# Layer 1's weight sums begun behind its own key rotation, and three reordered stretches, in a two-layer encoder step

## What is computed

```
z = rmsnorm(x) @ w_in        # [B | C | xin] conv, [c_q | c_kv | k_rope] attention, [gate_a | gate_b]
y_a = B * causal_conv3(C * xin)
y_b = latent attention of 8 heads with a rotary key, chunk-causal mask
x = x + rmsnorm((sigmoid(gate_a) * y_a + sigmoid(gate_b) * y_b) @ w_o)
x = x + rmsnorm(relu(rmsnorm(x) @ w1)^2 @ w2)
```

## Time and profile before

| what | value |
|---|---|
| median of 3 runs | 1724.19 us (1723.59 to 1724.62) |
| profiled execution | 1722.68 us |
| its span | 1720.9 us |
| TensorE busy | 1700.8 us (99%) |
| VectorE busy | 1324.4 us (77%) |
| ScalarE busy | 868.5 us (50%) |
| GpSimd busy | 142.8 us (8%) |
| DMA: SyncE's queue, GpSimd's queue | 32.2%, 16.4% of the 16 DMA engines' time |

### The profile page before, as it was taken

How to read it: one execution, slowest core, us unless ns; L and a number is a source line. 1 busy time by engine, 2 the same in 40 slices (tenths; PEclk the granted TensorE clock), 3 DMA queues, 4 the chain that set the end, 5 groups by cost and what they waited for, 6 DMA issues and landing times.

```text
span 1720.9 us, 31921 instructions
## 1 busy us (share of the span) xinstructions
PE 1700.8 (99%) x12687; PEld 1684.6 (98%) x12687; DVE 1324.4 (77%) x2538; ACT 868.5 (50%) x1681; POOL 142.8 (8%) x191
## 2 busy tenths in 40 slices
PE   9999999998999999999999999999999999999997
PEld 9999999998999999999999999999999999999997
DVE  7778877777798776668687788777878887777665
ACT  7635454554554454446366364545545536444452
POOL 1421222222000022100001000000000000000000
PEclk9999999999999999999999999999999999999998
DMA  7888888898412488733133234343623313322231
GB/s 239 209 186 183 224 208 219 200 245 241 124 64 70 133 191 180 160 91 106 62 103 133 96 112 132 116 137 108 205 106 99 99 39 109 98 87 86 75 99 56
DMA packets 91733, 233.65 MB, mean 136 GB/s; under 512 B 10304, under 2 KB 21824, under 8 KB 91584
## 3 DMA queue, kind: packets, MB, share of 16 engines
q1 hardware_dynamic: 69184, 179.16, 32.2%
q0 software_dynamic: 21120, 50.34, 16.4%
q10 hardware_dynamic: 1280, 2.10, 0.3%
HBM read 221.20 MB, written 60.69 MB: 164 GB/s over the span
## 4 chain that ended last, share of the span: by engine, by line
PE 90%; DVE 6%; DMA 2%; ACT 1%; issue 1%; SPq 0%; DVEq 0%; ACTq 0%
PE ring L820 18%; PE ring L822 18%; PE ring L821 18%; PE att L820 11%; PE att L822 11%; PE att L821 11%; DVE w_lo L2142 1%; PE att L3683 1%; DMA w_raw<-blocks_in 1%; DVE xs_lo L2561 1%; DMA my<-my_kept 1%; PE att L815 1%; PE att L814 1%; PE att L827 0%; DVE cv L2511 0%
## 5 line engine op out<-in xcount | busy, mean ns | idle before, releaser
L820 PE MATMUL ring<-xs_hi,w_lo 128*128 128x288 f32 x1792 | 532.9, 297 | 2.9 <-issue 1.2
L822 PE MATMUL ring<-xs_hi,w_hi 128*128 128x288 f32 x1792 | 527.9, 295 | 0.0
L821 PE MATMUL ring<-xs_lo,w_hi 128*128 128x288 f32 x1792 | 527.7, 294 | 0.0
L2142 DVE TENSOR_TENSOR w_lo<-w_raw,w_hi 128x1024 fp32r<-128x1024 f32 (+1 forms) x370 | 377.8, 1041 | 34.0 <-ACT w_hi L1227 22.9
L820 PEld LDWEIGHTS ring<-xs_hi,w_lo 128*128 128x128 f32 x1792 | 336.6, 188 | 6.0 <-issue 3.0
L821 PEld LDWEIGHTS ring<-xs_lo,w_hi 128*128 128x128 f32 x1792 | 336.8, 188 | 1.3
L822 PEld LDWEIGHTS ring<-xs_hi,w_hi 128*128 128x128 f32 x1792 | 336.6, 188 | 0.0
L822 PE MATMUL att<-f_hi,w_hi 128*128 128x288 f32 x960 | 283.2, 295 | 0.0
L821 PE MATMUL att<-f_lo,w_hi 128*128 128x288 f32 x960 | 282.9, 295 | 0.0
L820 PE MATMUL att<-f_hi,w_lo 128*128 128x288 f32 x960 | 282.6, 294 | 0.0
L820 PEld LDWEIGHTS att<-f_hi,w_lo 128*128 128x128 f32 x960 | 180.4, 188 | 0.0
(11 more groups left out here) (357 smaller groups left out, 3263.0 us busy)
## 6 DMA issues: line engine op xcount, KB each, us to landing
w_raw<-blocks_in SPq DMA_DIRECT2D x189, 512.0 KB, 3.9
weight_sums<-blocks_in POOLq DMA_DIRECT2D x96, 256.0 KB, 6.8
w_raw<-blocks_in SPq DMA_DIRECT2D x70, 256.0 KB, 4.0
w_raw<-weight_sums SPq DMA_DIRECT2D x52, 256.0 KB, 3.9
weight_sums<-blocks_in POOLq DMA_DIRECT2D x24, 512.0 KB, 5.2
weight_sums<-weight_sums POOLq DMA_DIRECT2D x48, 256.0 KB, 7.4
w_raw<-weight_sums SPq DMA_DIRECT2D x22, 512.0 KB, 4.1
small_raw<-small_in SPq DMA_DIRECT2D x16, 320.0 KB, 4.0
```

The costliest lines, as they stand in the source:

```text
L820: pe.matmul(out, w[1], x[0], start=first, stop=False)
L821: pe.matmul(out, w[0], x[1], start=False, stop=False)
L822: return pe.matmul(out, w[0], x[0], start=False, stop=last)
L2142: return dve.tensor_tensor(out, a, hi.bitcast(F32), ALU.subtract)
```

## The change

GpSimd makes layer 0's twelve sums around layer 0's key rotation as before, then waits for layer 1's key rotation, and behind that makes layer 1's twelve sums in one batch; the wait for the feed-forward pair is gone. ScalarE, head 2: the copy of the absorbed query goes behind the high parts of positions 4 and 5. ScalarE, samples: the second square comes ahead of weight 5, the turned tile 0 ahead of the third square, the small weights after the fifth. VectorE, head 2: `turned_lo` moves ahead of `block_gated` and `second_sum`. VectorE, head 7: one tap goes ahead of `upper_left`, the other behind `probabilities` and `first_difference`. VectorE, samples: `s_max(0)` comes right behind weight 4's low part, the caches' low parts follow it, the merged rows' second part is spread between `wo_out_a(0)` to `(2)`, `s_max(1)` comes ahead of weight 5's low part, and the small weights' low part moves behind `wo_add(0, 4)`. No instruction is added or removed on any engine.

```diff
--- before.py
+++ after.py
@@ -170,7 +170,6 @@
 
 N_SUMS = DEPTH * 2 * MIXED
 BEFORE_KEYS = 2
-FIRST_SUMS = 3 * MIXED
 
 
 def my_row(pl, k):
@@ -1187,19 +1186,21 @@
             nc.gpsimd.tensor_tensor(pl.kpe[:, cs], pl.rope1_t[:, :], pl.rx[:, cs], ALU.mult) \
                 .then_inc(pl.key_roped, 1)
 
-        pool.wait_ge(pl.x_landed[7], 16)
-        sums_copy(0)
-        sums_steps(0, BEFORE_KEYS, 0, 2 * MIXED)
         for L in range(DEPTH):
+            first, end = 2 * MIXED * L, 2 * MIXED * (L + 1)
+            if L == 0:
+                pool.wait_ge(pl.x_landed[7], 16)
+                sums_copy(0)
+                sums_steps(0, BEFORE_KEYS, 0, end)
             pool.wait_ge(pl.tables_landed, L * 32 + 32)
             key_rope(L, 0)
             key_rope(L, 1)
             if L == 0:
-                sums_steps(BEFORE_KEYS, FIRST_SUMS + 2, 0, FIRST_SUMS)
-                pool.wait_ge(pl.sums_third, 16 * FIRST_SUMS)
-                pool.wait_ge(pl.ring_full, full(0, r_pair(2, 1, 0)))
-                sums_copy(FIRST_SUMS)
-                sums_steps(FIRST_SUMS, N_SUMS + 2, FIRST_SUMS, N_SUMS)
+                sums_steps(BEFORE_KEYS, end + 2, 0, end)
+            else:
+                pool.wait_ge(pl.sums_third, 16 * first)
+                sums_copy(first)
+                sums_steps(first, end + 2, first, end)
         for i, (m0, m1) in enumerate(TAIL_MOVED):
             pool.wait_ge(pl.tail_factored, i + 1)
             nc.gpsimd.tensor_tensor(pl.x[:, m0:m1, cols(1)], pl.x[:, m0:m1, cols(1)], pl.last[:, m0:m1, :], ALU.add) \
@@ -1645,9 +1646,9 @@
                     block_kept(0)
                     pos_hi(L, at + 3)
                     block_kept(1)
-                    absorbed_hi(h)
                     pos_hi(L, at + 4)
                     pos_hi(L, at + 5)
+                    absorbed_hi(h)
                     pos_hi(L, at + 6)
                     exponents(h)
                     snapshot(1)
@@ -1777,16 +1778,16 @@
 
             s_exp(0)
             wo_square(0)
+            wo_square(1)
             wo_hi(5)
-            small_hi(L, HEADS)
-            wo_square(1)
+            s_turned_hi(0)
             wo_square(2)
-            s_turned_hi(0)
             wo_square(3)
             s_exp(1)
             wo_hi(6)
             s_turned_hi(1)
             wo_square(4)
+            small_hi(L, HEADS)
             wo_hi(7)
             s_context_hi(0)
             wo_square(5)
@@ -2505,9 +2506,9 @@
                 dve.memset(pl.u[:, 0:2], 0.0)
                 dve.tensor_copy(pl.u[:, 2 + NP_:4 + NP_], pl.const(C_STATE + L * (2 * KC) + 2 * h, 2))
 
-            def conv_taps(h):
+            def conv_taps(h, taps=(1, 2)):
                 eng.wait_ge(pl.conv_first, of_head(h, 1, 0))
-                for tap in (1, 2):
+                for tap in taps:
                     own.step(dve.scalar_tensor_tensor(out=pl.cv[:, :], in0=pl.u[:, tap:tap + NT + 2],
                                                       scalar=conv_weight(pl, L, h // 2, h % 2, tap), in1=pl.cv[:, :],
                                                       op0=ALU.mult, op1=ALU.add))
@@ -2762,9 +2763,9 @@
                     first_difference(1)
                     conv_taps(h)
                     pos_lo(L, at + 7)
+                    turned_lo(h)
                     block_gated()
                     second_sum(1)
-                    turned_lo(h)
                     own.wait()
                     lower_left(1, pl.ga[:, cols(0)])
                     small_lo(h + 1)
@@ -2836,10 +2837,11 @@
                     pos_lo(L, at + 5)
                     row_maxima(h)
                     absorbed_lo(h, pl.rest)
+                    conv_taps(h, (1,))
                     upper_left(1, pl.gb[:, cols(0)])
-                    conv_taps(h)
+                    probabilities(h)
                     first_difference(1)
-                    probabilities(h)
+                    conv_taps(h, (2,))
                     second_sum(1)
                     pos_lo(L, at + 6)
                     pos_lo(L, at + 7)
@@ -2912,11 +2914,10 @@
 
             for k in range(4, HEADS):
                 merged_lo(x_part(L, X_WOA + k), k, cols(0))
-            weight_lo(L, n_wo(4), SLOT_WO[4])
-            cache_lo(2, pl.nal[:, :, :], pl.naraw[:, :, :], pl.nah[:, :, :])
-            cache_lo(3, pl.n4l[:, :], pl.att[:, 1536:1792], pl.n4h[:, :])
-            for k in range(HEADS):
-                merged_lo(x_part(L, X_WOB + k), k, slice(NH, NP_))
+
+            def merged_b_lo(k0, k1):
+                for k in range(k0, k1):
+                    merged_lo(x_part(L, X_WOB + k), k, slice(NH, NP_))
 
             def s_max(t):
                 eng.wait_ge(pl.s_scored, L * 4 + t + 1)
@@ -2973,25 +2974,31 @@
             def wo_lo(m):
                 weight_lo(L, n_wo(m), SLOT_WO[m])
 
+            wo_lo(4)
             s_max(0)
+            cache_lo(2, pl.nal[:, :, :], pl.naraw[:, :, :], pl.nah[:, :, :])
+            s_normed(0)
+            cache_lo(3, pl.n4l[:, :], pl.att[:, 1536:1792], pl.n4h[:, :])
+            merged_b_lo(0, 3)
             wo_out_a(0)
-            s_normed(0)
+            merged_b_lo(3, 6)
             wo_out_a(1)
-            small_lo(HEADS)
+            merged_b_lo(6, HEADS)
             wo_add(0, 0)
             wo_out_a(2)
+            wo_add(0, 1)
+            s_turned_lo(0)
+            wo_out_a(3)
+            s_max(1)
             wo_lo(5)
-            wo_add(0, 1)
-            wo_out_a(3)
-            s_turned_lo(0)
+            s_normed(1)
             wo_add(0, 2)
-            s_max(1)
             wo_add(0, 3)
-            s_normed(1)
+            s_turned_lo(1)
             wo_lo(6)
             wo_out_a(4)
-            s_turned_lo(1)
             wo_add(0, 4)
+            small_lo(HEADS)
             wo_lo(7)
             wo_out_a(5)
             s_context_lo(0)
```

## The result

The changed kernel took 1738.26 us (median of 6 runs, 1735.52 to 1741.31), the kernel before 1724.08 us beside it (6 runs). The ratio is 1.0078 (95% interval 1.0061 to 1.0094): slower by 0.6 to 0.9%, 14.2 us by the medians. The forecast was 1728.7 us and at most 1736.0; the sign came as forecast, the size did not. The profiled execution took 1735.52 us, with a span of 1733.7 us.

The account below looks back on a forecast made before the run. TensorE was taken to bound the kernel. Gains of -10.2 us, stall of +12.7 and clock of +2.0 gave +4.5 us on the 1724.19 us median: 1728.7 us, range 1713.5 to 1736.

Parts of the forecast that it names:

- The reading of the page: Profile slices: TensorE's digit 9 in all 40; DMA share 7 to 9 in slices 1 to 10, 3 to 4 in 21 to 28.
- The gains: Filled TensorE holes in both layers: 10.2 us won, bounds 5.8 and 10.7.
- Heads 2 and 7: Both layers: reordered ScalarE and VectorE work shrinks TensorE's holes, gaining 1.4 us in head 2 and 1.8 in head 7.
- Layer 0's transfers: Sums leaving busy DMA stretches: 2.4 us from the kept-row load hole at 385 to 401, 0.7 from feed-forward holes.
- The samples: Both layers: the new vector order brings the softmax maximum 2.3 us earlier; 3.9 us won, bounds 2.0 and 4.2.
- The price: Layer 1's sums start late and stall TensorE 12.7 us in all, tightest at head 6's first, sum 8; clock 2.0 more.
- the pace of the sums in layer 1: Sums follow at 23.65 us a step, taken from layer 0's heads, against a reader at 20.6 us.
- The front of the batch: Layer 1's sums: from first copy to first third addition, 59.8 us, the middle of 56.7 and 62.8.
- C: Rival: long stall of 21 us from slow start and slow landings, clock falling twice; 1739 us, typically 1735; chance 0.10.
- The queue behind the wait: Later weight loads, small weights and a merged row's store queue behind SyncE's wait, wanted 10 us or more later.
- Rival B: The sums keep up in layer 1 at 22.0 us a step or less, no stall: 1714.0 us; chance 0.27.
- The clock: TensorE's clock falls behind the long stall; coming back costs about 2.0 us, bounds 0 and 4.

Follow-up runs that it names:

- the run without waits: The changed kernel, but layer 1's heads load plain weight blocks of the same size; SyncE waits for no sums, GpSimd still makes them: 1711.35 us, ratio 0.9933.
- six and six: The changed kernel with layer 1's sums split: six in layer 0's feed-forward stage, six behind layer 1's key rotation: 1711.30 us (0.9943), again 1714.29 us (0.9949).
- the orders alone: The changed kernel with its new ScalarE and VectorE orders, but the weight sums scheduled as in the kernel before: 1713.69 us, ratio 0.9950.

## Why the prediction was right or wrong

**The reading of the page.** "TensorE's digit is 9 in all 40" is not what the earlier trace rows show: slice 10, where layer 0's heads end, has an 8, and the last a 7. The windows behind it found the holes all the same. The DMA digits of layer 1's heads are 2 to 4, not 3 to 4.

**The gains: right, a little small.** 10.2 us were forecast; the profile leaves 11.3, and the run without waits gained 11.5 by its ratio. Heads 2 and 7: 3.2 forecast, 3.3 measured. Layer 0's transfers: 3.1 forecast; the spans of six and six (1709.4) and of the orders alone (1712.2) differ by 2.8. The samples were the term that was too small: 3.9 against 5.7, with its interval reaching down to 3.6. Two things can hide in the difference, the kept-row hole above and the clock (last section).

**The price: right in kind, 9 us too small.** The forecast had 12.7 + 2.0 = 14.7 us, the profile 24.1. The step that failed is the pace of the sums in layer 1, 23.65 us a step forecast, 24.9 measured. "Further sums follow at (264.9 - 75.7) / 8 = 23.65 us, taken from layer 0's heads, whose weight loads are those of layer 1". The front of the batch came as worked out: from the first copy to the first third addition 59.9 us (59.8 forecast). The first nine third additions of layer 1 in GpSimd's queue, in the changed kernel and in the run where nothing waits for sums:

```profile
L1144 POOL DMA_DIRECT2D weight_sums<-weight_sums x9: 805/807/840, 965.5 to 1164.6; - x9
```

```profile
L1149 POOL DMA_DIRECT2D weight_sums<-weight_sums x9: 805/807/837, 970.6 to 1161.7; - x9
```

That is 24.9 us a step where SyncE waits, and 23.9 where it does not. Eight steps at 24.9 are 199.1 us in place of 189.2, 10 us late; the landing of 4.6 us in place of 6.1 gives 1.5 back. So sum 8 was there at 1169.2. The forecast, moved by the 8.0 us by which layer 1 began earlier (912.29 to 904.26), said 1160.8.

It is tempting to put this on SyncE, whose bursts behind each wait cross the transfers that make the next sum. The run without waits speaks against it. Its last third addition of the nine, alone, landed in

```profile
DMA to landing us min/median/max: 7.1/7.1/7.1
```

so sum 8 was there at 1161.7 + 7.1 = 1168.8, only 0.4 us sooner. Counted from each batch's first copy (905.65, and 908.15 without waits), the way to sum 8 was 255.1 us in the forecast, 263.5 in the changed kernel and 260.7 without waits (62.4 to the first third addition, 191.2 for the steps, 7.1 for the landing). By one profile of each, 5.6 of the 8.4 us came with no wait at all, and 2.8 can belong to the waits. Why layer 1's heads make sums more slowly than layer 0's stays open.

The stall by the forecast's working is 12.7 + 8.4 = 21.1 us, against 18.7 of standing still and 5.4 of slow clock, in part of which TensorE works. The bound of 21 us stood in the text, but the range was cut at "C's nearer half", 1736.0. Of the rivals C came nearest, a long stall and the clock falling more than once, to which I had given a tenth; but C reached its 21 us by a slow start and slow landings, and neither came (59.9 and 4.6 us), so that its stall is near the measured one is in part luck.

**The queue behind the wait: wrong too.** "Queued behind SyncE's wait are all later weight loads, the small weights and the store of a merged row, wanted 10 us or more later". SyncE waited for odd sums as well as even ones, and behind sums 3 and 7 the small weights came so late that TensorE stood 5.0 and 8.7 us for them; between the two it stood 3.8 us for a half block of the same burst. The forecast looked at the one tightest reader and priced the others as contained in it. They were, nearly: with the small weights ahead the time is some 4 us less by the ratios, since sum 8 then holds TensorE itself.

**Rival B** needed 22.0 us a step. Not even the feed-forward stage makes that, whose own loads are lighter: with all twelve sums there, the first nine third additions came at

```profile
L1145 POOL DMA_DIRECT2D weight_sums<-weight_sums x9: 802/807/837, 645.4 to 826.6; - x9
```

22.65 us a step. So between the three runs the pace changes by no more than a tenth, 22.65, 23.9 and 24.9 us. The Trainium skill, "DMA: Bandwidth & Descriptors", in its anatomy of a transfer on GpSimd's path, gives 2.0 us plus bytes over 436 KB per us, by which I estimate 2.6 us for a link of 256 KB; the profile page of the changed kernel has a median of 7.0 us for the 48 that add one sum's half to another, and the measurement decides.

**The clock: right in kind, too small.** 2.0 us forecast for one fall, 5.4 measured for three, 1.8 each. The Trainium skill, "TensorE: Matmul & The Clock Gate", on HAM oscillation, has TensorE start cold behind such DMA waits; the trace agrees for the stalls of 3.8, 5.0 and 8.7 us: behind them the matmuls go 0.24 us apart in place of 0.13, which is 1.2 GHz, for 3.4, 5.4 and 4.4 us. Behind the stall of 3.8 us TensorE ran 0.9 us at full clock first. Behind that of 0.5 us nothing fell.

## What to carry to other kernels

A producer in batches and its reader are two clocks: compare their steps over the whole batch, allow for an error in a pace taken from another stage (5% here, 10 us over eight steps), and keep one item of slack, which here was worth 23 us. When a wait is put into a queue that issues in order, list what is queued behind it at every such wait, not only at the tightest: in the burst that followed here the last load took 15.94 us to land, and an engine that copies in order passed that on. Work that is moved out of a busy stage is not free in the next one: all twelve sums in the feed-forward stage opened three holes, six opened none.

## What was not expected of the hardware

**A hole of 2.8 us halved the clock in one profile and not in another.** The kernel before kept 1.00 through the hole at layer 0's samples. With the orders of heads 2 and 7 alone, the same hole (2.8 us, waiting for the same operand) shows in windows of TensorE as

```profile
412.00:416.00 4.00, 1.83 (x14) 1.00 1.05 247
416.00:420.00 4.00, 3.38 (x16) 0.62 0.61 175
420.00:424.00 4.00, 4.00 (x33) 0.95 0.57 67
```

16 matmuls in 3.38 us, some 1.3 us more than at full clock. So this hole cost 2.8 us in one execution and 4.1 in the other, and filling it can be worth more than its idle time. The mean granted clock of every run, to three decimals, fits that: 0.9971 over the 36 later runs of the kernel before, 0.9968 over the 11 with the orders of heads 2 and 7 alone, which all keep the hole, and 0.9979 over the 9 with the samples' orders alone. The difference of 0.0008 is 1.4 us of 1720, by this estimate most of the 1.8 us by which the samples' term was too small. Which runs had the fall is not shown.

**Loads land later beside the sums, and later again when SyncE issues them in bursts.** The half blocks (256 KB each) that SyncE loads from 960 to 1200 landed, in the kernel before, in the run without waits and in the changed kernel, in that order, in

```profile
DMA to landing us min/median/max: 2.4/3.4/4.5
```

```profile
DMA to landing us min/median/max: 2.6/5.8/10.2
```

```profile
DMA to landing us min/median/max: 2.6/8.7/13.5
```

The traffic adds 2.4 us to the median and the bursts another 2.9, though the DMA share is lower with them (0.80 against 0.86). Only the last of the three kernels has stalls there of more than 0.4 us in all, so later landings alone cost TensorE nothing as long as the loads were issued ahead.
